# Block two: another order of the attention's heads, and two of them prepared in parts inside stick breaking

## What is computed

```python
proj = h_res @ w_in[l]                       # fq fk fv f_logit | sq sk sv | c_q c_kv k_rot | mq | gate
out_fox = causal_softmax_attention(fq, fk, fv, head_scale, cumsum(log_sigmoid(f_logit + b)))
out_sb  = stick_breaking_attention(sq, sk, sv, head_scale)     # log_sigmoid, reversed cumsum over keys, exp
out_mla = causal_softmax_attention(q_full, k_full, v_mla, mla_scale)      # head width 64 + 32
out_mem = softmax(mq @ mk.T * head_scale) @ mv                            # 256 keys, no mask
y = (concat(out_fox, out_sb, out_mla, out_mem) * silu(gate)) @ w_out[l]
h_res = layer_norm(alpha * h_res + y)
```

## Time and profile before

| | |
|---|---|
| median of 3 runs | 4635.68 us (4626.44 to 4645.21) |
| the profiled execution | 4638.04 us |
| its span, first to last instruction | 4636.2 us |
| mean granted TensorE clock | 0.931 |
| busy | PE 3963.0 us (85%), DVE 2696.5 (58%), ACT 1535.0 (33%), POOL 1585.4 (34%) |
| stick breaking, layers 0 and 1 | 3346.50 to 3496.60, 4176.50 to 4323.70 us |
| attention of block two, layers 0 and 1 | 3501.40 to 3680.00, 4328.40 to 4508.00 us |

### The profile page before, as it was taken

The page is one execution under the profiler, slowest core; times in us unless marked ns, Lnnn a source line. Parts: engine busy times, 40 slices in busy tenths (PEclk is TensorE's granted clock), DMA queues, the critical chain, the costliest instruction groups (busy, mean ns, idle before and its releaser), DMA issues. The chain is left out here.

```text
span 4636.2 us, 105362 instructions
## 1 busy us (share of the span) xinstructions
PE 3963.0 (85%) x44052; PEld 3102.0 (67%) x44052; DVE 2696.5 (58%) x4470; ACT 1535.0 (33%) x2705; POOL 1585.4 (34%) x1260
## 2 busy tenths in 40 slices
PE   5999788877998699978985998599779789977887
PEld 4878688845666587768883776478536567853566
DVE  3466355556657447555555665765566567557656
ACT  1233233324552133323333553300256521015553
POOL 2233144412116323324441113655132165523315
PEclk7999999989999799989997999699889999988898
DMA  5445533352237445543325135433502463341236
GB/s 188 158 168 185 178 80 84 84 203 57 63 73 220 151 151 189 198 143 84 85 61 166 46 87 167 169 102 106 168 7 68 117 197 100 108 161 31 59 75 199
DMA packets 572997, 572.35 MB, mean 123 GB/s; under 512 B 151112, under 2 KB 470748, under 8 KB 570516
## 3 DMA queue, kind: packets, MB, share of 16 engines
q1 hardware_dynamic: 445012, 488.22, 34.8%
q10 hardware_dynamic: 127616, 78.95, 5.9%
HBM read 378.80 MB, written 192.42 MB: 123 GB/s over the span
## 5 line engine op out<-in xcount | busy, mean ns | idle before, releaser
L1096 PE MATMUL pr_acc<-hH,pr_wh 128*128 128x512 f32 (+1 forms) x1288 | 483.0, 375 | 0.0
L1097 PE MATMUL pr_acc<-hL,pr_wh 128*128 128x512 f32 (+1 forms) x1288 | 466.8, 362 | 0.0
L1098 PE MATMUL pr_acc<-hH,pr_wl 128*128 128x512 f32 (+1 forms) x1288 | 466.4, 362 | 0.0
L2720 ACT ACTIVATE an_p<-an_p,an_stat 128x1280 f32<-128x1280 f32 (+5 forms) x372 | 339.8, 915 | 153.6 <-DVE an_stat L2777 149.3
L2464 POOL TENSOR_TENSOR an_kl<-an_k,an_kh 128x1280 fp32r<-128x1280 f32 (+3 forms) x36 | 80.3, 2231 | 802.7 <-DVE an_qh L2454 786.0
L2674 PE MATMUL an_t<-ident,an_p 128*128 128x128 f32 x2152 | 312.6, 281 | 37.8 <-ACT an_pT L2727 27.0
L2773 DVE CUSTOM_DVE_ANT_0 an_p<-an_s,an_mask 128x256 f32<-128x256 f32 (+8 forms) x308 | 275.2, 894 | 102.7 <-PE an_s L2657 61.4
L1465 POOL TENSOR_TENSOR sp_sl<-sp_w,sp_sh 128x512 fp32r<-128x512 f32 x172 | 246.0, 1437 | 197.4 <-DVE sp_sh L1540 179.0
L2674 PEld LDWEIGHTS an_t<-ident,an_p 128*128 128x128 f32 x2152 | 237.2, 141 | 112.6 <-ACT an_pT L2727 51.5
L1140 POOL TENSOR_TENSOR pr_wl<-pr_w,pr_wh 128x1024 fp32r<-128x1024 f32 x58 | 142.7, 2460 | 471.7 <-DVE pr_wh L1160 471.7
L2004 DVE TENSOR_TENSOR rk_tu<-rk_tu,rk_ps 128x512 f32<-128x512 f32 x300 | 188.9, 683 | 194.0 <-PE rk_ps L1828 194.0
(11 more groups left out here) (378 smaller groups left out, 9778.4 us busy)
## 6 DMA issues: line engine op xcount, KB each, us to landing
CHK<-ri_out SPq DMA_DIRECT2D x24, 1920.0 KB, 8.1
rk_in<-CHK SPq DMA_DIRECT2D x240, 128.0 KB, 2.5
pr_w<-in_w_in ACTq DMA_DIRECT2D x58, 512.0 KB, 4.5
UT<-pr_out SPq DMA_DIRECT2D x45, 640.0 KB, 4.6
sp_w<-in_w_in ACTq DMA_DIRECT2D x50, 512.0 KB, 5.2
U<-sp_c SPq DMA_DIRECT2D x100, 256.0 KB, 2.0
mod_w<-in_w_mod SPq DMA_DIRECT2D x16, 1024.0 KB, 7.9
mo_w<-in_w_out SPq DMA_DIRECT2D x16, 1024.0 KB, 10.9
```

The lines of the kernel that those rows point to most:

```text
L1096: nc.tensor.matmul(out, wh[:, u, k, 0:m], hi, start=(k == 0), stop=False)
L1097: nc.tensor.matmul(out, wh[:, u, k, 0:m], lo, start=False, stop=False)
L1098: ins = nc.tensor.matmul(out, wl[:, u, k, 0:m], hi, start=False, stop=(k == KT - 1))
L2720: nc.scalar.activation(row, row, ACT.Exp, bias=stat[:, n % NPM, j, 1:2], scale=heads[groups[n][0]].scale, accum_out=total[:, sum_column(n, ...
```

## The change

The heads' order becomes 2 of the memory, 4 latent, 4 forget, 2 of the memory. The first two, which are prepared inside stick breaking, are thus heads of the memory. Their `upper` moves to steps 3 and 9; `lower` is cut in two, keys and half of the queries at steps 5 and 11, the other half at steps 6 and 12. `forget_rows` is gone from stick breaking. The sums' column of a head goes by the row of its output and so keeps its place.

```diff
-    def lower(self, pool, x):
-        u, head, g = x % self.NQB, self.heads[x], self.core.nc.gpsimd
-        c, nk, nq = head.kv % 2, self.kvs[head.kv].nk * P, head.nq * P
+    def lower_k(self, pool, x):
+        head = self.heads[x]
+        c, nk = head.kv % 2, self.kvs[head.kv].nk * P
         pool.wait_ge(self.hi.sem, self.hi.nth(x + 1))
         if x:
             pool.wait_ge(self.lo.sem, self.lo.nth(x))
...
+    def lower_q(self, x, cols):
+        u, head = x % self.NQB, self.heads[x]
         rows, to = (slice(0, head.d), self.qB) if self.shape[x] == "long" else (slice(HD, P), self.qH)
-        g.tensor_tensor(to[rows, u, 0:nq], self.qT[rows, u, 0:nq], self.qH[rows, u, 0:nq], ALU.subtract).then_inc(self.lo.sem, 1)
+        return self.core.nc.gpsimd.tensor_tensor(to[rows, u, cols], self.qT[rows, u, cols], self.qH[rows, u, cols], ALU.subtract)
+
+    def lower(self, pool, x):
+        self.lower_k(pool, x)
+        self.lower_q(x, slice(0, self.heads[x].nq * P)).then_inc(self.lo.sem, 1)
+
+    def lower_first(self, pool, x):
+
+        self.lower_k(pool, x)
+        self.lower_q(x, slice(0, self.heads[x].nq * P // 2)).then_inc(self.lq.sem, 1)
+
+    def lower_second(self, pool, x):
+
+        pool.wait_ge(self.lq.sem, self.lq.nth(x + 1))
+        cols = self.heads[x].nq * P
+        self.lower_q(x, slice(cols // 2, cols)).then_inc(self.lo.sem, 1)
...
+        rank = [sum(other.row < head.row for other in heads) for head in heads]
...
-            return groups[n][0] * (NT // len(heads)) + spec[n][j][0] - q_first
+            return rank[groups[n][0]] * (NT // len(heads)) + spec[n][j][0] - q_first
...
-    ahead_at = NS - 6
+    upper_at = {t: 3 + 6 * t for t in range(following.ahead)}
+    lower_at = {step + 2: t for t, step in upper_at.items()}
...
-                    if 0 <= st - ahead_at < following.ahead:
-                        following.forget_rows(act, st - ahead_at)
...
-                    if 0 <= st - ahead_at < following.ahead:
+                    if st in lower_at:
                         pool.wait_ge(rs.sem, rs.nth(unit(st, 0)))
-                        following.lower(pool, st - ahead_at)
-                        pool.wait_ge(following.lo.sem, following.lo.nth(st - ahead_at + 1))
+                        following.lower_first(pool, lower_at[st])
+                        pool.wait_ge(following.lq.sem, following.lq.nth(lower_at[st] + 1))
+                    if st - 1 in lower_at:
+                        pool.wait_ge(rs.sem, rs.nth(unit(st, 0)))
+                        following.lower_second(pool, lower_at[st - 1])
+                        pool.wait_ge(following.lo.sem, following.lo.nth(lower_at[st - 1] + 1))
...
-                    if 0 <= st - ahead_at < following.ahead:
-                        following.upper(dve, st - ahead_at)
+                    for t in range(following.ahead):
+                        if upper_at[t] == st:
+                            following.upper(dve, t)
...
-        for more, their in ((latent_heads, latent_kvs), (mem_heads, mem_kvs)):
-            heads += [head._replace(kv=len(kvs) + head.kv) for head in more]
-            kvs += their
+        parts = [(mem_heads[0:2], mem_kvs), (latent_heads, latent_kvs), (heads, kvs), (mem_heads[2:4], mem_kvs)]
+        heads, kvs = [], []
+        for more, their in parts:
+            for head in more:
+                heads.append(head._replace(kv=len(kvs)))
+                kvs.append(their[head.kv])
```

More of the change, by code:

```diff
@@ L2406, in __init__ @@
         self.hi, self.lo, self.lk = core.counter("an_heads"), core.counter("an_split"), core.counter("an_k_split")
+        self.lq = core.counter("an_q_half_split")
         self.au, self.qk, self.vt = core.counter("an_forget_rows"), core.counter("an_scores"), core.counter("an_v_turned")
@@ L2463, in lower @@
             rows = slice(0, {"twice": P, "forget": HD, "long": head.d}[self.shape[x]])
-            g.tensor_tensor(self.kL[rows, c, 0:nk], self.kT[rows, c, 0:nk], self.kH[rows, c, 0:nk], ALU.subtract).then_inc(self.lk.sem, 1)
+            self.core.nc.gpsimd.tensor_tensor(self.kL[rows, c, 0:nk], self.kT[rows, c, 0:nk], self.kH[rows, c, 0:nk], ALU.subtract) \
+                .then_inc(self.lk.sem, 1)
             pool.wait_ge(self.lk.sem, self.lk.nth(sum(self.opens[0:x + 1])))
+    def lower_q(self, x, cols):
+        u, head = x % self.NQB, self.heads[x]
         rows, to = (slice(0, head.d), self.qB) if self.shape[x] == "long" else (slice(HD, P), self.qH)
-        g.tensor_tensor(to[rows, u, 0:nq], self.qT[rows, u, 0:nq], self.qH[rows, u, 0:nq], ALU.subtract).then_inc(self.lo.sem, 1)
+        return self.core.nc.gpsimd.tensor_tensor(to[rows, u, cols], self.qT[rows, u, cols], self.qH[rows, u, cols], ALU.subtract)
[9 more added lines that the diff above has]
+        self.lower_q(x, slice(cols // 2, cols)).then_inc(self.lo.sem, 1)
     def forget_rows(self, act, t):
@@ L2794, in _ @@
                 V_.tensor_copy(rcpT[:], T2[0:NT, len(o.uses) % 2 * 512:len(o.uses) % 2 * 512 + P]).then_inc(rc.sem, 1)
-    counts = [(zeroed, 3), (hi, len(heads)), (lo, len(heads)), (lk, sum(opens)), (au, aug_no[-1]), (vt, vturns_to(len(kvs) - 1)), (qk, NS), (mxs, NS), (mx, NS),
+    counts = [(zeroed, 3), (hi, len(heads)), (lo, len(heads)), (lk, sum(opens)), (inputs.lq, inputs.ahead), (au, aug_no[-1]), (vt, vturns_to(len(kvs) - 1)), (qk, NS), (mxs, NS), (mx, NS),
               (ex, NS), (tg, len(o.turns)), (pv, len(o.weighs)), (oo, NG), (rc, 3), (sums_out, 1), (neg, int(any_bias)), (given_back["ACT"], o.given["ACT"]),
```

## The result

The changed kernel takes 4605.24 us (median of 4 runs, 4602.27 to 4608.52) against 4635.76 us before (median of 4 as well): ratio 0.9931, 95% interval 0.9919 to 0.9943, so 0.69% faster. The forecast was 4600 us, 0.77% faster. The profiled execution took 4602.27 us; its span is 35.8 us shorter than before. A second set of runs gave 4595.79 us and the ratio 0.9928 [0.9911, 0.9944].

The account below looks back on a forecast made before the run. The prediction took TensorE (PE) to bound stick breaking and the attention. Terms of -21.9 + 2 + 4.5 - 2.8 + 0.3 = -17.9 us per layer took 4638.0 to 4602.2, less 2.4 for the median: about 4600, range 4581 to 4622.

Parts of the forecast that it names:

- Late preparation: Stick breaking, steps 18 and 19: removing the preparation there saves 21.92 and 21.83 us in the two layers.
- Early preparation: Stick breaking, preparation added from step 3 on: mostly hidden in idle time, +2 us per layer.
- lock rival: Stick breaking: POOL parts block DVE for their whole run, 6.2 us per layer instead of 2; 4608 us, chance 0.19.
- the lower end: Early preparation's bounds are 0 and four stalls, 11.8 us per layer; the estimate stayed near 0, at +2.
- The attention: Opening +4.5, end -2.8 and two more forget heads +0.3 us, together +2.0 per layer.
- The opening's term: Attention's start: PE runs short of work before head 2, +4.5 us per layer, between 1.7 and 10.
- The bare opening: Attention's start: PE idles 4 us and the clock falls for 10 us; +9 us per layer, 4618 us, chance 0.14.
- The end: Attention's end: two memory heads close it instead of four, -2.8 us per layer, between -5.6 and 0.
- DMAs: Four fewer issues at stick breaking's start, four more in the attention: cost 0, uncovered 1.3 us per layer.
- The two more forget heads prepared inside the attention: Attention: extra ACT casts and longer POOL key parts, taken as +0.3 us per layer, between 0 and 6.2.
- The sum: All terms over stick breaking and attention: -17.9 us per layer, -35.8 us for both layers.

Follow-up runs that it names:

- order_alone: Kernel before with the new order of heads, both heads still prepared whole at steps 18 and 19; 4626.73 us, ratio 0.9989 to the kernel before.
- both_wide: Kernel both, with copies moved to steps 6 and 18 and POOL's parts to 8, 9 and 20, 21; ratio 0.9897 to the kernel before.
- zero_memset: Changed kernel, with POOL zeroing its running sum by a memset instead of adding two tiles of zeros; ratio 0.9916 to the kernel before.
- both: Changed kernel with POOL's running sum zeroed by memset and a latent head in second place; 4572.61 us, ratio 0.9871 to the kernel before.
- early_alone: Changed kernel's early, split preparation with the old order of heads, forget heads first, forget rows at steps 3 and 9; ratio 0.9932 to the kernel before.
- copies_lead: Kernel before with one edit: DVE's copies two steps earlier, at 16 and 17, POOL's work staying at 18 and 19; ratio 0.9957.

## Why the prediction came out right

*Late preparation, -21.9 per layer predicted, -22.2 / -22.1 measured.* Taking it as the difference from steps 6 and 7 was sound. The text laid the stall on POOL's waiting and working, without weighing them. The runs weigh them: 12.2 us come back with the copies' place, the remaining 9.9 only when POOL's pieces are shorter or lie elsewhere too. ACT's forget rows, which this term holds as well, were not taken out alone; without them, and with short heads, `order_alone` still takes 29.4 us. I had not weighed them well even afterwards: for the new order alone I expected 26 us in these steps, and they took 29.4 to 30.1, because a short head leaves the wait as it was.

*Early preparation, +2 predicted, +1.6 measured* in steps 3 to 13. Those steps also hold the second pair's part; 1.0 us lies in steps 4 and 5 and 0.6 in steps 9 to 13. The lock rival (each POOL part holds DVE, and PE, for as long as it runs, 6.2 us per layer) has the mechanism right and the size wrong: of the 7.7 us that POOL's pieces run, softplus is held for 2.9, and PE loses 1.6. The reason for staying near the lower end does not carry: the 2.48 us in the earlier trace rows are two operations, so the new pieces, of 0.72 to 1.60 us, are not half as long. And 2.94 us was too much for a stall of this kind, since 1.81 us of that hole stay when the hold is gone. The Trainium skill, "SBUF — State Buffer", section "Who interferes with whom", says that a VectorE instruction with two SBUF inputs contends with a GpSimd instruction that reads SBUF and not with one that only writes it. Both halves agree here: 0.78 and 1.25 us instead of 0.29 beside the pieces, and 0.69 us beside the memset where it was 1.11 beside the addition.

*Steps 20 to 22, not predicted, +1.25 per layer.* I had let them go unchanged. In the changed kernel PE waits 1.03 us for softplus ahead of step 23. The three steps take 16.04 us in `before`, `order_alone` and `both_wide`, which stall at 18 and 19, and 17.2 to 17.3 in all the others. The reading that fits is that DVE and ACT ran ahead while PE stood, and that this lead is gone with the stall; no run tries it by itself.

*Steps 14 and 15, not predicted, -1.06 / +1.70.* The hole of 2.94 us is the same before and after; what differs is the granted clock behind it. After the change it is the 3.40 us at 0.55 in the stretches above, in layer 1 alike. Stretches of the kernel before, layer 0 and layer 1, and of `both_wide`, layer 0, as above:

```profile
3426.00:3432.80 6.80, 5.53 (x9) 2.86 (x10) 4.03 (x12) 2.97 (x7) 1.07 (x1) 0.50 0.01 1
4257.00:4263.80 6.80, 6.71 (x30) 3.40 (x32) 4.74 (x16) 3.78 (x10) 0.91 (x2) 1.00 0.00 0
...
3422.40:3425.80 3.40, 3.40 (x6) 1.58 (x6) 2.36 (x8) 1.69 (x5) 0.00 (x0) 0.50 0.00 0
```

Over all profiles the two steps follow the clock. With the hole of 2.94 us they take 11.6 us in the three layers without half clock behind it, 13.0 to 13.3 in the ten with 3.4 us of it, and 14.3 to 14.7 in the five with 6.8. With the hole of 1.81 us they take 10.48 us in the four layers of `zero_memset` and `both`, which have none, and 12.1 in the two of `both_wide`, which have 3.4 us. So the clock behind that hole, not the change, makes the two layers' figures differ, and of the 2.8 us that the memset took off these steps only 1.1 is the shorter hole.

*The attention, +2.0 predicted, +0.9 / +1.4 measured.* These come from one execution of either kernel; over all profiles the attentions of this order take 175.6 to 180.6 us (mean 178.0) and the six of the old order 177.9 to 179.2 (mean 178.4), so not even the sign is shown. The opening's term was sized too small in one place: head 2 was to be ready 19.7 us after the first score, and was at 21.8. I took 6 us for the scores of head 0 from rows at a clock of 1.00, although the same text has the opening at 0.50; the load was issued at 7.9 us. The chain from there took 13.95 us against 13.7. The bare opening, a rival of 0.14 that asked for 4 us of idle time, came halfway: 2.7 and 2.2 us of holes, and in one layer 13.7 us of clock at half. The end went as foreseen and somewhat better: the last two heads take 11.87 us from the last copy-out of the head before them, in place of 18.67. PE is idle for 1.6 us there and was for 5.6, so by idle time the term is -4.0 and not -2.8.

*DMAs, predicted at 0:* steps 0 to 2, which have the fewer issues, differ by 0.25 us in either direction. The two more forget heads prepared inside the attention can't be told apart from its other differences; that term stays untested.

*The sum.* -17.9 per layer was predicted, -19.8 / -15.9 measured. The large term was right by its mechanism. That the spans' difference is the predicted 35.8 us to the tenth is luck: of the two layers' clock at step 15, of the attention's scatter, and of the stretches outside the two stages. The medians say 30.5.

What stays open: the 1.81 us of hole at step 14 that are left with the memset. PE waits for softplus there, DVE for ACT's logarithm, and ACT, for 2.48 us, for DVE's `negatives` of the same step. The hole is thus a turn of DVE, ACT and DVE; no run here shortens it.

## What to carry to other kernels

When one engine's piece reads what another writes, put the writer a step or two ahead in its own list. A wait inside an in-order list holds everything behind it: here 12 of 22 us came back with two moved lines, while the new order of the heads alone gave 3 to 4. Before moving a piece into an engine's idle time, look at what the engine beside it does at that moment, and price every chain at the clock of its own stretch.

## What the runs showed of the hardware that was not expected

The hold is exact. In every stretched 128x128 row above, VectorE's operation ends 0.15 or 0.16 us after GpSimd's, however long that was: 3371.73 behind 3371.57 in the changed kernel, 3372.02 behind 3371.87 in `early_alone`, 3436.35 behind 3436.20 in `copies_lead`, 3443.48 behind 3443.33 in `both_wide`. Over the twelve profiles 151 stretched operations of softplus of this size do so, and 169 of 128x512 end 0.55 us after GpSimd's. The end of a held row thus tells when the other engine was done, plus a rest that goes by the row's own size; its duration tells nothing of its work.

The granted clock fell after holes that were small each. In layer 1's opening PE was still busy for 9.83 of 12.00 us, and the next 12.00 us, without a hole, were granted 0.51; layer 0, with PE less busy (9.30), kept 1.00. Nor did a hole decide it alone: behind the same 1.81 us at step 14 the clock stayed at 1.00 in four layers and was at half for 3.4 us in two.
